# Turning the expert rows with 32x32 blocks on VectorE, the activations inside the gate products, and a new pairing and order of the 24 expert blocks

## What is computed

```python
t = rmsnorm(x, norm_ffn_g)                       # 1088 tokens x 1024
lg = t @ w_rg + b_rg ; le = t @ w_re + b_re      # 4 groups, 32 experts
# best group, best 2 of its 8 experts; gate = softmax(top 2) * softmax(lg)[group]
a = einsum('td,edf->tef', t, w_gate)             # d = 1024, f = 256
b = einsum('td,edf->tef', t, w_up)
act = silu(a) * b * comb
y = einsum('tef,efd->td', act, w_down)           # x += y
```

## Time and profile before

| | |
|---|---|
| median of three runs | 1276.28 us |
| the profiled execution | 1268.7 us, of which the span is 1266.9 us |
| expert stage in the span | 963 to 1262 us, 24 blocks |
| busy TensorE / VectorE / ScalarE / GpSimd | 92% / 53% / 26% / 12% of the span |
| mean granted clock of TensorE | 0.968 |
| HBM traffic | 172.60 MB read, 42.36 MB written |

### The profile page before, as it was taken

The page is one execution under the profiler, slowest core; times in us unless marked ns, Lnnn a source line. Parts: engine busy times, 40 slices in busy tenths (PEclk is TensorE's granted clock), DMA queues, the critical chain, the costliest instruction groups (busy, mean ns, idle before and its releaser), DMA issues.

```text
span 1266.9 us, 17480 instructions
## 1 busy us (share of the span) xinstructions
PE 1168.5 (92%) x6415; PEld 594.5 (47%) x6415; DVE 675.2 (53%) x2085; ACT 323.1 (26%) x934; POOL 146.8 (12%) x159
## 2 busy tenths in 40 slices
PE   6988879999999999998999999999787999999995
PEld 3434536545555555553555565556442333333331
DVE  1118689999999999831345454545554222222220
ACT  1124434443453456421111111111110101110110
POOL 0000000000000000300000000000001223333332
PEclk9997899999999999999999999999897999999997
DMA  8871000030000002357110011000587998999992
GB/s 317 306 252 46 1 1 26 17 150 34 1 34 34 1 26 114 151 205 312 33 51 23 28 50 50 34 1 34 207 355 311 397 336 319 364 378 385 387 332 53
DMA packets 48914, 194.89 MB, mean 154 GB/s; under 512 B 12240, under 2 KB 15094, under 8 KB 36515
## 3 DMA queue, kind: packets, MB, share of 16 engines
q1 hardware_dynamic: 37883, 173.79, 35.3%
q0 software_dynamic: 10368, 17.87, 5.8%
q10 hardware_dynamic: 576, 2.10, 0.4%
HBM read 172.60 MB, written 42.36 MB: 170 GB/s over the span
## 4 chain that ended last, share of the span: by engine, by line
PE 50%; DVE 4%; DMA 2%; issue 1%; ACT 0%; POOL 0%; SPq 0%; POOLq 0%; DVEq 0%
PE bank L1401 13%; PE bank L843 9%; PE bank L1347 9%; PE bank L1408 7%; PE bank L1325 3%; PE bank L1285 2%; PE bank L1388 2%; PE bank L1126 1%; DMA W<-in_w_mo 1%; DMA W<-in_cache_mem_k 1%; PE bank L1204 1%; DVE G L1848 1%; PE bank L1431 1%; DMA W<-z_scratch,idx_i 1%; PE bank L849 1%
## 5 line engine op out<-in xcount | busy, mean ns | idle before, releaser
L843 PE MATMUL bank<-W,G 128*128 128x512 f32 (+1 forms) x768 | 314.6, 565 | 3.8 <-DVE G L1848 3.0
L1904 DVE SCALAR_TENSOR_TENSOR W<-W,dwT 128x128 f32<-128x128 f32 (+1 forms) x1048 | 271.8, 335 | 0.0
L843 PEld LDWEIGHTS bank<-W,G 128*128 128x128 f32 x768 | 145.4, 192 | 151.0 <-issue 147.6
L1401 PE MATMUL bank<-W 128*32 128x512 f32 x1152 | 155.8, 595 | 1.0 <-DVE W L2430 0.9
L1347 PE MATMUL bank<-W 128*128 128x512 f32 x256 | 115.2, 599 | 0.2 <-DVE W L2309 0.2
L715 POOL TENSOR_SCALAR st<-st 128x1 f32<-128x1 f32 (+3 forms) x40 | 13.7, 343 | 874.7 <-DVE st L2005 434.1
L1126 PE MATMUL bank<-W 128*128 128x512 f32 x256 | 111.8, 594 | 0.0
L2430 DVE TENSOR_TENSOR W<-bank,cvec 128x512 f32<-128x512 f32 x48 | 31.0, 686 | 145.7 <-PE bank L1388 145.7
L1401 PEld LDWEIGHTS bank<-W 128*32 128x32 f32 x1152 | 43.7, 110 | 82.5 <-issue 80.9
L1408 PE MATMUL bank<-W 128*32 128x512 f32 x576 | 81.7, 602 | 0.5 <-ACT W L1795 0.5
L1126 PEld LDWEIGHTS bank<-W 128*128 128x128 f32 x256 | 47.9, 190 | 57.4 <-issue 56.9
(11 more groups left out here) (324 smaller groups left out, 1467.3 us busy)
## 6 DMA issues: line engine op xcount, KB each, us to landing
W<-in_w_exp_gate SPq DMA_DIRECT2D x23, 1024.0 KB
W<-in_w_exp_up SPq DMA_DIRECT2D x23, 1024.0 KB
W<-in_w_exp_down SPq DMA_DIRECT2D x23, 1024.0 KB
G<-in_w_exp_gate SPq DMA_DIRECT2D x9, 1024.0 KB
G<-in_w_exp_up SPq DMA_DIRECT2D x9, 1024.0 KB
G<-in_w_exp_down SPq DMA_DIRECT2D x9, 1024.0 KB
W<-in_cache_mem_k SPq DMA_DIRECT2D x8, 1024.0 KB, 5.0
W<-in_cache_mem_v SPq DMA_DIRECT2D x8, 1024.0 KB, 7.8
```

Source lines behind the costliest of these rows:

```text
L843: mm = pe.matmul(bank[0:rows, at:at + hi - lo], HT[:, c, 0:rows], w[:, c, lo:hi], start=(c == 0), stop=(c == DC - 1))
L1401: mm = pe.matmul(B[2 + par][lo:hi, :], HG[par][:, c, lo:hi], WGU[u][:, :, c, :], start=(c == 0), stop=(c == DC - 1), skip_group_check=True)
L1904: dve.scalar_tensor_tensor(y, src, w, y, ALU.mult, ALU.add).then_inc(M["conv_tap"], 1)
```

## The change

Five things change together.

1. The rows of all blocks from the third on (`TURNED = 2`) are no longer turned by TensorE. POOL gathers them in quarters: four indirect DMAs per block, each with 128 pieces of 1 KB, so that partition 32s+i gets the piece s of row i. VectorE then turns each quarter with one `transpose` of 32x32 blocks straight into `HG` (`turn_segments`). POOL waits for `hg_ready` in place of `zt4_done` ahead of the next gather, and adds block n-1 in the same pass as it gathers block n+3.
2. The 2 transposes of the activations move from behind the gate products to their middle, from block 4 on.
3. The gain of the norm is applied where `Z3` is written. It is loaded as 128 copies of its 4 KB row (`GB`), and `H3` and `HG` become plain copies. The features keep their own order in `Z3` and in the router weights.
4. 28 small products (`place_segments`) and a conversion on VectorE make the table `seg_i` of the pieces.
5. Which experts share a block, and the order of the blocks, are changed. The count of blocks, of rows and of weight bytes is the same.

```diff
-BLOCKS = [0, 20, 1, 21, 22, 15, 11, 16, 2, 7, 3, 13, 14, 12, 23, 8, 4, 9, 19, 17, 18, 5, 10, 6]
...
+BLOCKS = [0, 7, 1, 15, 8, 2, 13, 11, 3, 16, 17, 12, 18, 19, 14, 20, 21, 4, 22, 9, 23, 5, 10, 6]
...
+QMAX = max(max(c) for c in CAPS)
+TURNED = 2
...
-        HG = [view(W, ROUT + 2048 + 1024 * r, DC, 128) for r in range(2)]
+        HG = [view(W, ROUT + 2048 + 1024 * r, 4, DC, 32) for r in range(2)]
         YB = [view(W, ROUT + 4096 + 1024 * r, D) for r in range(2)] + [view(W, ROUT + 1024, D)]
+        GB = view(W, 12288, D)
...
+        def quarters_of(n):
+
+            return [(q0 + k) * NE + rank_of(g, j) for g, j, q0, count in COLUMNS[BLOCKS[n]] for k in range(count)]
+
+        def rows_landed(n):
+
+            return 16 * n + 16 if n < TURNED else 16 * TURNED + 64 * (n + 1 - TURNED)
+
+        def rows_turned(n):
+
+            return 2 * n + 2 if n < TURNED else n + 1 + TURNED
+
+        ROWS0 = rows_landed(NB - 1)
...
+                    sp.wait_ge(M["mkb_used"], DEC_B)
+                    sp.dma_start(GB, i["norm_ffn_g"].to_broadcast([128, D])).then_inc(M["gb_in"], 16)
...
+                if u == 4:
+                    sp.wait_ge(M["z3_ready"], AFTER["z3_ready"] + NT)
                 load_down(sp, expert_id(NEED[u]), u)
...
+            z3_segments = z3_d.rearrange("t (s f) -> (t s) f", s=4)
+
+            def gather_quarters(n):
+
+                for q, col in enumerate(quarters_of(n)):
+                    pool.indirect_dma_start(out=ZG[:, 256 * q:256 * q + 256], out_offset=None, in_=z3_segments,
+                                            in_offset=bass.IndirectOffsetOnAxis(ap=seg_i[:, col:col + 1], axis=0),
+                                            bounds_check=4 * NTOK - 1, oob_is_err=False).then_inc(zg_in, 16)
...
             gather(idx_i[:, BLOCKS[0]:BLOCKS[0] + 1], zg_in, ZG)
+            pool.wait_ge(M["zt4_done"], 2)
             pool.wait_ge(M["route_ready"], 2)
-            for n in range(NB + 3):
-                if n + 1 < NB:
-                    pool.wait_ge(M["zt4_done"], 2 * n + 2)
-                    at = BLOCKS[n + 1]
-                    gather(idx_i[:, at:at + 1], zg_in, ZG)
-                if n == 3:
+            gather(idx_i[:, BLOCKS[1]:BLOCKS[1] + 1], zg_in, ZG)
+            pool.wait_ge(M["zt4_done"], 2 * TURNED)
+            pool.wait_ge(M["route_ready"], 3)
+            gather_quarters(TURNED)
+            for n in range(NB + 1):
+                if n + 3 < NB:
+                    pool.wait_ge(M["hg_ready"], rows_turned(n + 2))
+                    gather_quarters(n + 3)
+                if n == 1:
                     pool.wait_ge(M["gate_ready"], 1)
                     for k in range(4):
                         pool.wait_ge(x2_out[k], 16 * len(range(k, NT, 4)))
-                if n >= 3:
-                    add_block(n - 3)
-            pool.wait_ge(zg_in, 16 * NB)
-            pool.wait_ge(M["zt4_done"], 2 * NB)
+                if n >= 1:
+                    add_block(n - 1)
...
+            def place_segments():
+
+                for q in range(QMAX):
+                    for s in range(4):
+                        mm = pe.matmul(B[7][PART * s:PART * s + PART, NE * q:NE * q + NE], TABLE[0:2 * NE, PART * q:PART * q + PART], PERM[0:2 * NE, :], start=True, stop=True, skip_group_check=True)
+                mm.then_inc(M["r_cols"], 1)
+
             pe.wait_ge(M["r_tt"], AFTER["r_tt"] + 1)
             place(B[3], 0)
+            place_segments()
...
+            def turn_activation(n):
+
+                p = n % 2
+                pe.wait_ge(M["ab_ready"], n + 1)
+                if n == 3:
+                    pe.wait_ge(M["r_taken"], AFTER["r_taken"] + 1)
+                for c in range(2):
+                    mm = pe.transpose(B[4 + p][:, c * 128:(c + 1) * 128], AB[p][:, c * 128:(c + 1) * 128], ident)
+                mm.then_inc(M["at_done"], 1)
+
+            def gate_up(tiles, par, upper=0, within=-1):
+
                 for c in range(DC):
                     if c == DC // 2 and upper:
                         pe.wait_ge(M["hg_ready"], upper)
+                    if c == DC // 2 and within >= 0:
+                        turn_activation(within)
                     for lo, hi, u in tiles:
-                        mm = pe.matmul(B[2 + par][lo:hi, :], HG[par][:, c, lo:hi], WGU[u][:, :, c, :], start=(c == 0), stop=(c == DC - 1), skip_group_check=True)
+                        mm = pe.matmul(B[2 + par][lo:hi, :], HG[par][:, lo // PART, c, :], WGU[u][:, :, c, :], start=(c == 0), stop=(c == DC - 1), skip_group_check=True)
...
-                    pe.wait_ge(M["hg_ready"], n * 2 + 4)
+                    pe.wait_ge(M["hg_ready"], rows_turned(n + 1))
                     weights_of(n + 1, wgu_in, 32, WGU_AFTER)
 
                     if n:
                         pe.wait_ge(M["ab_ready"], n)
-                    gate_up(tiles_of(n + 1), 1 - p).then_inc(M["gu_done"], 1)
-                pe.wait_ge(M["ab_ready"], n + 1)
-                if n == 3:
-                    pe.wait_ge(M["r_taken"], AFTER["r_taken"] + 1)
-                for c in range(2):
-                    mm = pe.transpose(B[4 + p][:, c * 128:(c + 1) * 128], AB[p][:, c * 128:(c + 1) * 128], ident)
-                mm.then_inc(M["at_done"], 1)
-                if n + 2 < NB:
-
-                    for mm in turn_rows(n + 3):
-                        mm.then_inc(M["zt4_done"], 1)
+                    gate_up(tiles_of(n + 1), 1 - p, 0, n if n > 3 else -1).then_inc(M["gu_done"], 1)
+                if n <= 3 or n + 1 == NB:
+                    turn_activation(n)
...
-                    dve.tensor_scalar(by_row(Z3[0:n3, :], DC), XB(s3)[0:n3, :].rearrange("p (f c) -> p f c", c=DC), st[0:n3, 41:42], None, ALU.mult).then_inc(M["z3_ready"], 1)
+                    if s3 == 0:
+                        dve.wait_ge(M["gb_in"], AFTER["gb_in"] + 16)
+                    dve.scalar_tensor_tensor(Z3[0:n3, :], XB(s3)[0:n3, :], st[0:n3, 41:42], GB[0:n3, :], ALU.mult, ALU.mult).then_inc(M["z3_ready"], 1)
...
-                        dve.tensor_tensor(H3[:, 4 * half:4 * half + 4, 0:n3], src, gain(V_FFN + 4 * half, 4, n3), ALU.mult).then_inc(M["h3_ready"], 1)
+                        dve.tensor_copy(H3[:, 4 * half:4 * half + 4, 0:n3], src).then_inc(M["h3_ready"], 1)
...
-                    dve.tensor_tensor(buf[:, 4 * half:4 * half + 4, :], B[half][:, :].rearrange("p (c t) -> p c t", c=4), gain(V_FFN + 4 * half, 4), ALU.mult).then_inc(ready, 1)
+                    dve.tensor_copy(buf[:, :, 4 * half:4 * half + 4, :], B[half][:, :].rearrange("p (c q t) -> p q c t", c=4, q=4)).then_inc(ready, 1)
+
+            def turn_segments(n):
+
+                dve.wait_ge(zg_in, rows_landed(n))
+                for q in range(4):
+                    a = dve.transpose(HG[n % 2][:, q], ZG[:, 256 * q:256 * q + 256].rearrange("p (f c) -> p c f", c=DC))
+                a.then_inc(M["hg_ready"], 1)
...
-                    take_rows(None, HG[p], M["zt4_done"], n * 2 + 5, M["hg_ready"])
+                    turn_segments(n + 2)
...
-            take_rows(None, HG[0], M["zt4_done"], 1, M["hg_ready"])
-            take_rows(None, HG[1], M["zt4_done"], 3, M["hg_ready"])
+            take_rows(HG[0], M["zt4_done"], 1, M["hg_ready"])
+            dve.wait_ge(M["r_cols"], AFTER["r_cols"] + 1)
+            dve.tensor_scalar(seg_i, B[7][:, 0:QMAX * NE], 4.0, seg, ALU.mult, ALU.add).then_inc(M["route_ready"], 1)
+            take_rows(HG[1], M["zt4_done"], 3, M["hg_ready"])
```

43 lines of the change are left out of this document (24 added, 19 removed), and 10 rows, old and new, of the table COLUMNS.

## The result

The changed kernel takes 1296.01 us as the median of four runs (1293.29 to 1301.59), the kernel before 1275.67 us beside it (1271.91 to 1276.29). The ratio is 1.0181, with a 95% interval of 1.0154 to 1.0207: slower by 1.8%, some 23 us by the ratio; the two medians are 20.3 us apart. The profiled execution of the changed kernel took 1293.39 us with a span of 1291.6, against 1268.7 and 1266.9.

The account below looks back on a forecast made before the run. It took TensorE (92% busy) and the DMA engines as both nearly full. Late gather loops +16.9, the third block +4 and three terms of +0.5 made +22.4 on 1276.3 us, say 1298 us; range 1256 to 1326.

Parts of the forecast that it names:

- the main term: Expert stage: 17 blocks at 12.9 instead of 11.68 us, less 4 x 0.96 us, together +16.9 us.
- 864 packets per block: Queue q0: four indirect DMAs of 128 + 16 packets raise a block's count from 432 to 864.
- The first rival: Gather loop: 1 KB pieces take turns several at a time, loop under 10.72 us and hidden; 1258.6 us, chance 0.20.
- The two ends of the round: Loop of gather and turn: 10.7 us without weights in the queue, 19.0 us with weights always there.
- A mix of two kinds of rounds: Expert blocks: a third of contended loops at 19.0 us, the rest free at 10.72, giving 13.4 us a block.
- 12.9 us in 17 blocks, 10.72 in 4: Expert stage: some 17 blocks slowed to 12.9 us, about 4 at 10.72 where DMA share is 0.88.
- VectorE's turn: Four 128x256 transposes per block on VectorE, 0.41 us each, 1.6 us together.
- The third block, +4 us: Third block's gather: 576 packets beside weight loads land about 992 instead of 983.5 us, half hidden; +4 us.
- The router, +1 us: Router: 28 small products of `place_segments` at +0.5 us, `Z3` written from two inputs at +0.5 us.
- The copies of steps 0 to 3: Steps 0 to 3: copies to `AT` lose their cover, 4 x 0.47, at most 1.9 us; counted as +0.5.
- the fourth case: Expert loops contended more often, 14.9 us a block, or a falling clock; +70 us, about 1345 us, chance 0.08.
- The second rival: Expert stage: loop hidden, TensorE runs into the last weight load; 1272 to 1288, about 1277 us, chance 0.15.

Follow-up runs that it names:

- E1: Changed kernel with part 1 alone undone: TensorE turns the rows of all blocks, one gather of 4 KB rows per block; 1275.06 us, ratio 1.0014.
- E4: Changed kernel with each block's four VectorE transposes done twice; 1325.25 us, ratio 1.0416.
- E5: Changed kernel loading 1 MB of weights per expert where the change loads 3 MB; 1249.28 us, ratio 0.9827.
- E9: Changed kernel with a ring of seven quarter buffers for the gathered rows, a semaphore for each; 1266.06 us, ratio 0.9956.
- E7: Changed kernel with the pairing and order of blocks of the kernel before; 1292.13 us, ratio 1.0142.
- E8: Changed kernel with part 2 alone undone: activations turned behind the gate and up products in every block; 1292.42 us, ratio 1.0154.
- E10: Kernel before, loading 1 MB of weights per expert in place of 3; 1269.80 us, ratio 0.9986.
- E3: Changed kernel with a semaphore for each quarter, each fetched again as soon as VectorE has turned it; 1265.04 us, ratio 0.9950.
- E2: Changed kernel with one indirect DMA of 128 rows of 4 KB per block instead of four of 1 KB pieces; 1267.66 us, ratio 0.9951.

## Why the prediction was right, and where it was not

The forecast was 1298 us, 22.4 us more than before; the measured time is 1296.01, and the ratio gives some 23 us more. The cause was the one named, the round of gather and turn on one buffer, late while weights load: E1 takes the round away and the loss goes, E4 lengthens it and the loss grows, E5 takes two thirds of the weights away and the loss goes. The signs named for it are there: TensorE idle before `gate_up` until VectorE's transposes end, and VectorE idle until the gather lands. Several terms were wrong, though, and that they cancel to 2 us is luck. With the packet count alone put right, the round beside weights comes to 12.2 us (below), the main term to 17 x (12.2 - 11.68) - 3.8 = 5.0 instead of 16.9 us, and the forecast to 1287 us. Too many packets stood in for a hand-off of 0.8 us that the sum of the round leaves out, for a turn 0.6 us too short and for late rounds in 19 blocks instead of 17.

- *864 packets per block* is wrong. It is 432 + 48 = 480. The 128 pieces of a quarter make 32 packets, four pieces of 1 KB in each, and only the 16 completions come on top for each further DMA. The sizes bear this out: from 1238 to 1258 us, with no weights, the changed kernel moves 906 packets, 576 below 512 bytes and none from 512 bytes to 2 KB, though every piece has 1 KB. The first rival said just that pieces may take turns several at a time; the Trainium skill, "DMA: Bandwidth & Descriptors", section "Queues, rings and completion order", has whole packets of several descriptors per turn. On the several descriptors in a packet the trace agrees with the page, with 4 where it calls 9 to 17 typical; that a turn is one packet, no row here shows.
- *Yet the rival's conclusion was false*: the point from which it decides was a round of 10.72 us, and the loaded rounds took 13.17. With the true count, 192 packets, my own sum for a loaded round would have been 4.1 + 12 x (0.307 + 4 x 0.046) + 0.6 + 1.6 = 12.2 us, still above 10.72. So the count was wrong, but the round is long even with few packets, because the hand-off, the four issues and the turn (8.1 us together) are in it whatever the queue does.
- *The two ends of the round*, 10.7 and 19.0 us, should have been 9.7 and 14.8. Without weights the last quarter lands 1.6 us after its issue, not 3.9; that row belongs to a gather whose rows did not begin to move before. Both sums begin where GpSimd wakes and so leave out the 0.8 us from the end of the turn to that point. A mix of two kinds of rounds, the step that gave 13.4, is not what happens: the landing takes all values from 2.96 to 6.65 us, and no round beside weights runs at TensorE's pace. (The 14 turns of a free loop in that step come from no row.) TensorE's blocks do look like the sign that I gave, with 11.1 to 16.4 us and three above 15, but this is not two kinds of rounds.
- *12.9 us in 17 blocks, 10.72 in 4* came out as 13.17 us in 19 rounds and 9.7 in the last two. The term was +16.9 us and the rounds gave +24.4.
- *VectorE's turn* takes 2.2 us, 0.55 each (the row's mean of one is 610 ns as the records overlap), not 1.6. It lies in the round, so the 0.6 us are in every one. It is still inside the bounds of the earlier trace rows, but nearer to the strided `activate` than I took it.

```profile
L2490 DVE STREAM_TRANSPOSE W<-W 128x256 f32<-128x256 f32 x88 | 48.6, 610 | 204.6 <-DMA W<-z_scratch,WR 204.6
...
L2320 DVE SCALAR_TENSOR_TENSOR W<-G,st,W 128x1024 f32<-128x1024 f32 x8 | 10.2, 1277 | 2.8 <-POOL st L743 2.8
```

- *The third block, +4 us*, did not happen. Its gate and up products start at 990.17, against 987.99 in the trace of before, and the first gather had started 2.6 us later already. The 4 us made up for a part of what the main term lacked, by chance.
- *The router, +1 us*: `Z3` takes 1277 ns instead of 1334, so that term is 0. The router ended 2.6 us later in the changed kernel, but it does so by anything from -2.2 to +7.2 in kernels with the same code there, so this can't be told from chance, in either direction.
- *The block without the transposes*, 10.72 us, is 10.81 in E5 and E9; the 0.09 us more come with the two transposes amid the products. *The copies of steps 0 to 3* are exposed as said: their `down` waits 0.47 us after the copy to `AT`. *The order* is worth nothing (E7), and so is *part 2* under the loop (E8).
- *A falling clock* is there. After an idle time of 3.00 us the products take 1.09 us, which is the 1.2 GHz level, until 1109.4, and the granted clock is 0.96 in three of the six stretches from 985 to 1262 us. It costs nothing that shows here, since all 22 turns waited for their gather and TensorE waited for the turns. The price of +70 us that I gave the fourth case was for rounds that did not come.
- *Two smaller slips.* From 1050 to 1053 us q1 was not silent beside the 285 packets of the earlier trace rows; it moved 37 packets, 0.17 MB. No sum used this. And the lower end of the forecast's own range, 1262 us, does not follow from its terms: 12.0 us a block and the low ends of the small terms give about 1275.
- *The second rival* (weights bound, about 1277 us) is where the better versions end. E9 waits 2.67 and 4.01 us at the end, where the kernel before waited 1.53. Its stage is 6.8 us shorter than before, where I had put it 1 us longer: the 6.6 us of more DMA work were put for twice the packets, and there are 11% more.

What the change was made for, 21 us of TensorE, was thus lost in this way: with room on the DMA engines it brings 17.5 us (E10 against E5); with the weights' traffic some 11 of these are gone in every arrangement of buffers that was tried (E3 and E9 against before: 6.5 to 6.8 us of stage are left); and the serial round on one buffer costs another 28.6 us (changed against E3). E3 with all of the change takes 0.995 of the time of before; E9, at 0.9956, cannot be told from it.

## What to carry to other kernels

Work that is taken off the busy engine and put behind a DMA becomes part of that buffer's round: hand-off, issue, landing, use. Add that round up with the landing as it is beside the other traffic, and compare it with the pace that the engine would have. Chain the pieces (a semaphore for each quarter, reissue as soon as a piece is used) before looking for a second buffer, and if the DMA engines are full already, expect only a part of the gain (6.5 of 17.5 us here).

## What the hardware showed that was not expected

- Splitting one indirect DMA of 128 rows of 4 KB into four of 1 KB pieces leaves the number of data packets as it is, 128; only 48 completions are added. The split's own price is then GpSimd's three further issues, 1.0 us each and 0.3 between them, of which 2.5 us come back as a shorter landing (E2).
- The same 512 KB take 7.6 us to land after one issue (E2) and 5.1 after the fourth of four, as they move during the issues; 2.8 us with a third of the weights beside them, 1.6 without any.
- Work added to a late round is partly refunded: 2.2 us on VectorE cost 1.4 (E4), as the mean landing went from 5.1 to 4.3 us; that this comes of the weights' smaller share is a reading that fits, not one that was tested.
- A transpose of 128x256 in blocks of 32x32, float32, read with a stride of 8 elements, takes 0.55 us on VectorE, where `activate` (128x256, two inputs) takes 0.68.
